# Split products for the keys and values of a sparse attention mixer, with its indexer sums on GpSimd

## The reference

```python
def dsa_mixer(h, w_in, cq_g, ckv_g, w_uq, w_uk, w_uv):
    cq, ckv, qi, ki, wi = jnp.split(h @ w_in, C_SPLITS, axis=-1)      # 384, 256, 8 x 64, 64, 8
    q = (rmsnorm(cq, cq_g) @ w_uq).reshape(b, s, C_HEADS, C_NOPE)     # 8 heads of 128
    ckv = rmsnorm(ckv, ckv_g)
    ...
    rel = jax.nn.relu(jnp.einsum('bthd,bsd->bths', qi[:, i0:end], ki[:, :end]))
    score = jnp.einsum('bths,bth->bts', rel, wi[:, i0:end])
    _, idx = lax.top_k(jnp.where(admissible, score, -jnp.inf), kk)    # 64 keys of each query
    ...                                                               # softmax over those keys, values, out
```

## Time and profile before

| | |
|---|---|
| median of 3 runs | 1085.22 us (1082.76 to 1085.29) |
| the profiled execution | 1083.29 us, span 1081.6 us |
| granted clock of TensorE, mean | 0.999 of full |
| busy share: TensorE, VectorE, ScalarE, GpSimd | 99%, 72%, 52%, 6% |

### The profile page before, as it was taken

The page is one execution under the profiler, slowest core; times in us unless marked ns, Lnnn a source line. Parts: engine busy times, 40 slices in busy tenths (PEclk is TensorE's granted clock), DMA queues, the critical chain, the costliest instruction groups (busy, mean ns, idle before and its releaser), DMA issues.

```text
span 1081.6 us, 16046 instructions
## 1 busy us (share of the span) xinstructions
PE 1070.0 (99%) x6172; PEld 938.8 (87%) x6172; DVE 776.1 (72%) x1015; ACT 565.2 (52%) x816; POOL 70.1 (6%) x169
## 2 busy tenths in 40 slices
PE   9999999999999999999999999999999999999997
PEld 8888888999888888888888888888978988888886
DVE  5966769875896786676778667677487768676675
ACT  6534446667766753353465344345466676443442
POOL 3000010010020200000010000002100101000000
PEclk9999999999999999999999999999999999999999
DMA  8746474564254365554536564553804535745641
GB/s 320 255 189 221 167 273 131 171 198 130 77 187 165 108 248 195 219 176 174 194 117 252 200 229 159 190 194 109 273 14 143 176 117 195 252 161 189 225 163 40
DMA packets 50156, 194.59 MB, mean 180 GB/s; under 512 B 4497, under 2 KB 24481, under 8 KB 31793
## 3 DMA queue, kind: packets, MB, share of 16 engines
q1 hardware_dynamic: 48832, 189.54, 49.4%
q0 software_dynamic: 1264, 4.25, 1.3%
HBM read 192.73 MB, written 1.05 MB: 179 GB/s over the span
## 4 chain that ended last, share of the span: by engine, by line
PE 91%; DVE 4%; DMA 2%; ACT 2%; issue 1%; POOL 0%; SPq 0%; POOLq 0%; DVEq 0%; ACTq 0%
PE psum L1077 22%; PE psum L961 21%; PE psum L969 11%; PE psum L942 5%; PE psum L1299 3%; PE psum L1062 3%; PE psum L947 3%; PE psum L1290 1%; PE psum L981 1%; PE psum L785 1%; PE psum L786 1%; PE psum L787 1%; PE psum L1268 1%; PE psum L1154 1%; DVE w_ring L2363 1%
## 5 line engine op out<-in xcount | busy, mean ns | idle before, releaser
L2363 DVE TENSOR_TENSOR w_ring<-raw,w_ring 128x2048 fp32r<-128x2048 f32 (+1 forms) x119 | 270.4, 2272 | 23.3 <-ACT w_ring L1665 23.0
L1665 ACT ACTIVATE w_ring<-raw 128x2048 fp32r<-128x2048 f32 x121 | 230.7, 1906 | 47.1 <-DMA raw<-in_ffn_w_gate 23.8
L2480 DVE TENSOR_REDUCE work<-psum 128x256 f32<-128x512 f32 x172 | 114.4, 686 | 175.6 <-PE psum L969 161.4
L961 PE MATMUL psum<-h_both,w_ring 128*128 128x512 f32 x1024 | 237.3, 389 | 0.0
L961 PEld LDWEIGHTS psum<-h_both,w_ring 128*128 128x128 f32 x1024 | 192.2, 188 | 39.9
L1077 PE MATMUL psum<-w_ring,g_both 128*128 128x512 f32 x936 | 220.0, 390 | 0.0
L1077 PEld LDWEIGHTS psum<-w_ring,g_both 128*128 128x128 f32 x936 | 173.2, 188 | 34.3
L1778 ACT ACTIVATE V<-work 128x512 f32<-128x512 f32 x44 | 27.9, 634 | 251.0 <-DVE work L2489 251.0
L969 PEld LDWEIGHTS psum<-h_both,w_ring 128*128 128x128 f32 x1024 | 127.1, 192 | 2.5
L969 PE MATMUL psum<-h_both,w_ring 128*128 128x256 f32 x1024 | 127.9, 283 | 0.0
L2363 DVE TENSOR_TENSOR w_ring<-QT,w_ring 128x2048 fp32r<-128x2048 f32 x40 | 91.4, 2284 | 0.8 <-ACT w_ring L1665 0.8
(11 more groups left out here) (337 smaller groups left out, 1566.5 us busy)
## 6 DMA issues: line engine op xcount, KB each, us to landing
raw<-in_ffn_w_gate SPq DMA_DIRECT2D x43, 1024.0 KB, 4.8
raw<-in_ffn_w_up SPq DMA_DIRECT2D x43, 1024.0 KB, 4.8
QT<-in_ffn_w_down SPq DMA_DIRECT2D x40, 1024.0 KB, 4.8
raw<-in_ab_w_in SPq DMA_DIRECT2D x7, 1024.0 KB, 5.5
gain_row<-in_norm_g POOLq DMA_DIRECT2D x8, 512.0 KB, 6.1
raw<-in_ffn_w_down SPq DMA_DIRECT2D x4, 1024.0 KB, 4.7
raw<-in_xa_wk SPq DMA_DIRECT2D x4, 1024.0 KB, 4.8
raw<-in_ab_w_out SPq DMA_DIRECT2D x4, 1024.0 KB, 4.8
```

Of the source, the lines that this page charges most:

```text
L961: nc.tensor.matmul(outs[-1][:, :], hi[:, k, P * j:P * (j + 1)], h_both[:, k].rearrange("p a n -> p (a n)"), start=(k == 0), stop=False)
L1665: nc.scalar.activation(w_hi[:, c % RING, 0:k * n], raw_at(c)[:, 0:k * n], ACT.Copy)\
L2363: nc.vector.tensor_tensor(w_lo[:, c % RING, 0:k * n], raw_at(c)[:, 0:k * n], w_hi[:, c % RING, 0:k * n].bitcast(F32), ALU.subtract).then_i ...
L2480: nc.vector.tensor_reduce(dst[:, p % 2, TOK * j:TOK * (j + 1)], bank(name).rearrange("p (a n) -> p n a", a=2), AX.X, ALU.add)\
```

## The change

In the sparse mixer: `cuk` and `cuv` become chunks that are split like the others, and `keys` and `latent_values` form three fp32r products with split latents (`lat_hi` by ScalarE, `key_lo` by VectorE) in place of float32 ones; the chunk of keys' and values' latent, `c.1`, comes after the indexer's and is done tile by tile. `relevance` multiplies heads in 64-row halves of the array, two halves into two banks in turn, without zeros in the key. The sums of tile 1's relevance leave VectorE for GpSimd (`relevance_sums`), as does the low split of the first output chunk, `co.0` (`first_output_lo`). The order of the units' steps on TensorE, ScalarE and VectorE is another one. In the first mixer, `abo.2`'s high split on ScalarE moves behind the copies of `qc`, and half of its low split on VectorE moves behind `hn`. At boundary 2, VectorE's split of the next feed-forward's first chunk moves from between the two halves of `gained` to between the two halves of `input_lo`.

```diff
-    uk, uv = ([A[n][0, 4 * i:4 * (i + 1)].rearrange("h (k p) n -> p (h k) n", p=P) for i in range(2)]
-              for n in ('c_w_uk', 'c_w_uv'))
-    add("ca", *uq, uk[0], split=False)
-    add("cb", uk[1], *uv, split=False)
+    uk, uv = (A[n][0].rearrange("h (k p) n -> p (h k) n", p=P) for n in ('c_w_uk', 'c_w_uv'))
+    add("ca", *uq, split=False)
+    add("cuk", uk)
+    add("cuv", uv)
...
+            def relevance_sums():
+                pool.wait_ge(const_done, 3)
+                pool.wait_ge(ki_done, 1)
+                for i in range(4):
+                    pool.wait_ge(*freed[f"rel1.{i}"])
+                    for j in range(2):
+                        link(pool.tensor_scalar(rel1[:, i, j, :], rel1[:, i, j, :],
+                                                iw[:, 1, head_of(i, j):head_of(i, j) + 1], 0.0, ALU.mult, ALU.add))
+                    link(pool.tensor_tensor(rel1[:, i, 0, :], rel1[:, i, 0, :], rel1[:, i, 1, :], ALU.add))
+                    ins = pool.tensor_tensor(score[:, 1, :], rel1[:, i, 0, :], score[:, 1, :] if i else cmask[:, 1, :],
+                                             ALU.add)
+                    if i < 3:
+                        link(ins)
+                ins.then_inc(tile1_scored, 1)
...
+            def first_output_lo():
+                c = C["co.0"]
+                pool.wait_ge(split_hi, n_split[c])
+                for q in range(4):
+                    o = slice(CH // 4 * q, CH // 4 * (q + 1))
+                    ins = pool.tensor_tensor(w_lo[:, c % RING, o], raw_at(c)[:, o], w_hi[:, c % RING, o].bitcast(F32),
+                                             ALU.subtract)
+                ins.then_inc(split_lo, 1)
+
...
+            def relevance(t, m):
                 n = P * (t + 1)
-                up(f"rel{t}.{i}", [(slice(TOK * j, TOK * j + n),
-                                    [(qiT[:, i, P * t:P * (t + 1)], kiT[:, j, 0:n])]) for j in range(2)])
-
+                outs = [take(f"rel{t}.{2 * m + j}") for j in range(2)]
+                for i in range(2):
+                    for j in range(2):
+                        o = slice(64 * j, 64 * (j + 1))
+                        last = nc.tensor.matmul(outs[j][:, TOK * i:TOK * i + n], qiT[o, 2 * m + i, P * t:P * (t + 1)],
+                                                kiT[o, 0, 0:n], start=True, stop=True)
+                        if i:
+                            filled(f"rel{t}.{2 * m + j}", last)
...
             def keys(p):
-                w = resident(f"cuk_{p // 2}").rearrange("p (h k) n -> p h k n", h=4)
-                up(f"cuk.{p}", [(slice(TOK * j, TOK * (j + 1)),
-                                 [(w[:, 2 * (p % 2) + j, k, :], latT[:, 3 + k, :]) for k in range(2)])
-                                for j in range(2)])
+                w = weights(C["cuk"])
+                three_products(f"cuk.{p}", [(slice(TOK * j, TOK * (j + 1)),
+                                             [([a[:, 2 * (2 * p + j) + n, :] for a in w], key_latent(n))
+                                              for n in range(2)]) for j in range(2)])
 
             def latent_values(i, t):
-                w = resident(f"cuv_{i}").rearrange("p (h k) n -> p h k n", h=4)
-                up(f"cuv.{i}.{t}", [(slice(0, 512), [(tile(latT[:, 3 + k, :], t), w[:, :, k, :]) for k in range(2)])])
+                w = [a.rearrange("p (h k) n -> p h k n", k=2)[:, 4 * i:4 * i + 4] for a in weights(C["cuv"])]
+                three_products(f"cuv.{i}.{t}", [(slice(0, 512), [(key_latent(n, slice(P * t, P * (t + 1))),
+                                                                  [a[:, :, n, :] for a in w]) for n in range(2)])])
```

ScalarE's and then VectorE's order of the units' steps, from the third unit's copies and from the relevance sums on:

```diff
+            prob_copy(us[2])
+            prob_copy(us[3])
+            split_to(C["co.1"])
+            exps(us[4])
+            act.wait_ge(tile1_scored, 1)
             output_hi(us[2])
-            prob_copy(us[3])
-            exps(us[4])
+            output_hi(us[3])
             split_to(C["co.2"])
-            output_hi(us[3])
+            exps(us[5])
             prob_copy(us[4])
-            exps(us[5])
+            exps(us[6])
+            output_hi(us[4])
             split_to(C["co.3"])
             prob_copy(us[5])
-            exps(us[6])
-            output_hi(us[4])
...
-            for t, i in RELEVANCE:
-                relevance(t, i)
-            top_rounds(0, range(rounds))
+            relevance(0)
+            relevance(1)
+            split_to(C["cuk"])
+            split_to(C["cuv"])
+            latent("cckv", QL, QL + KVL)
+            relevance(2)
+            relevance(3)
+            top_rounds(0, range(2))
+            key_latent_lo()
+            top_rounds(0, range(2, rounds))
             top_mask(0)
             row_max(us[0])
-            top_rounds(1, range(0, 2))
+            row_max(us[1])
             normalise(us[0])
-            row_max(us[1])
-            top_rounds(1, range(2, 4))
             normalise(us[1])
-            top_rounds(1, range(4, 6))
+            dve.wait_ge(tile1_scored, 1)
+            top_rounds(1, range(0, 6))
+            output_lo(us[0])
+            top_rounds(1, range(6, 7))
+            output_lo(us[1])
+            top_rounds(1, range(7, rounds))
             row_max(us[2])
-            output_lo(us[0])
-            top_rounds(1, range(6, rounds))
-            normalise(us[2])
-            split_to(C["co.0"])
-            output_lo(us[1])
             top_mask(1)
             row_max(us[3])
+            normalise(us[2])
             normalise(us[3])
+            row_max(us[4])
+            nxt[0] = C["co.1"]
+            dve.wait_ge(split_lo, n_split[C["co.0"]])
             split_to(C["co.1"])
+            normalise(us[4])
             output_lo(us[2])
-            row_max(us[4])
-            normalise(us[4])
             output_lo(us[3])
             row_max(us[5])
             split_to(C["co.2"])
             normalise(us[5])
             row_max(us[6])
+            output_lo(us[4])
             split_to(C["co.3"])
-            output_lo(us[4])
             normalise(us[6])
             row_max(us[7])
             output_lo(us[5])
```

The moves of the first mixer, on ScalarE and on VectorE, and that of boundary 2 on VectorE:

```diff
-            split_to(C["abo.2"])
             for i in range(2):
                 act.wait_ge(*full(f"qc.{i}"))
...
+            split_to(C["abo.2"])
             act.wait_ge(mean_done, 1)
...
-            lo_part(C["abo.2"], 1)
             dve.wait_ge(vrstd_done, 1)
...
+            lo_part(C["abo.2"], 1)
...
-                        if s == 3 and half == 0:
+                        if s in (2, 3) and half == 0:
                             split_to(last + 2)
```

223 lines of the change are left out of this document (123 added, 100 removed).

## The result

The changed kernel takes 1087.67 us (median of 11 runs, 1085.98 to 1089.72) against 1083.54 us (11 runs, 1082.49 to 1085.96) of the kernel before: a ratio of 1.0036, 95% interval 1.0027 to 1.0044. It is slower, by some 4 us. The forecast was 1084.3 us and no difference beyond 0.3% as the likeliest; the time lies within its range of 1079 to 1089, on the slow side, but it moved beyond its interval where no difference was forecast.

What follows compares the result with a forecast made beforehand. The prediction took TensorE to bound the kernel, busy 1070.0 of 1081.6 us. Sparse mixer +0.4, first mixer +0.2 and boundary 2 -0.55 summed to about 0, giving 1084.3 us, range 1079.0 to 1089.0.

Steps and rivals of the forecast that it cites:

- What leaves TensorE: Sparse mixer's keys, values, transposes and relevance products: 5.4 us less TensorE work, or 2.8 if array halves do not overlap.
- The prediction's sign for this: Relevance products at 0.06 us a record of 256 columns if the array halves overlap, 0.11 to 0.12 if not.
- The sums on GpSimd: Tile 1's relevance sums end at 792.7 to 794.7 us, about when VectorE wants them at 794.1, without a stall.
- the third rival: GpSimd's tile 1 sums end late, at 803 us, and delay VectorE's tile 1 rounds: 1087.5 to 1093 us, chance 0.17.
- The upper half: Sparse mixer up to unit 3's transpose, taken at 807.5 us: nearly all kept, 5.4 less 1 us.
- The tail's chain: ScalarE and VectorE steps from unit 3's transpose at 807.5 us to unit 5's copy at 823.9: 16.4 us.
- What the tail costs: From unit 3's to unit 6's transpose TensorE idles some 5 us, 4 ahead of unit 5's values; unit 6's transpose at 830.5.
- the mixer's +0.4: Net change of the sparse mixer: the TensorE time saved is given back by idle time in its tail, +0.4 us.
- Both of the prediction's signs of being wrong: Wait ahead of unit 5's values under 2 us: faster; VectorE's first tile 1 round waiting over 3 us on GpSimd: slower.
- The first mixer's edits: TensorE's 1.35 us wait ahead of the `qc` products goes, but `raw` is freed later: +0.2 us, from -1.0 to +0.6.
- Boundary 2: TensorE's wait for `x_state` behind a split, ahead of 368.36 us, goes: -0.55 us.
- The sum: Sparse mixer +0.4, first mixer +0.2 and second boundary -0.55 us: about 0, so 1084.3 us.

Runs made afterwards that it cites:

- repairs_one_half: Changed kernel with unit 5's copy earlier, `co.0`'s low split later, first mixer's moves undone, all relevance products on rows 0 to 63: 1082.43 us, ratio 0.9992.
- late_low_split: Changed kernel with GpSimd's low split of `co.0` held until unit 1's probabilities are normalised: 1086.48 us, ratio 1.0017 to the kernel before.
- copy_ahead: Changed kernel with unit 5's copy on ScalarE ahead of unit 6's exponentials, `output_hi` of unit 4 and `co.3`'s high split: 1082.49 us, ratio 0.9986.
- rows_ahead: Changed kernel with unit 2's output rows back between unit 4's values and unit 5's transposes on TensorE: 1082.09 us, ratio 0.9986.
- fill_wait: Changed kernel with seven extra, unused float32 products in TensorE's wait ahead of unit 5's values: 1086.04 us, ratio 1.0021.

## Why the prediction was wrong

**What leaves TensorE**: right in kind, 1.3 us too large. Values take 1.47 us a call (forecast 1.37), two calls of keys 787.46 to 790.52, 1.53 each (1.44), and the four 6.0 together. The relevance products take 0.134 a record of 256 columns where 0.11 was assumed: three rows of the changed kernel,

```profile
772.37 0.72 PE L1556 MATMUL psum<-krT,shared 64*128 64x128 f32 x8
...
783.89 1.13 PE L1556 MATMUL psum<-krT,shared 64*128 64x256 f32 x8
784.96 2.86 PE L1331 MATMUL psum<-latT,w_raw 128*128 128x256 f32 x12
```

the last of them the start of what follows. Together all eight items take 3.4 us, so 2.0 are saved of the 2.7 taken; in all 0.9 + 0.9 + 0.2 + 2.0, some 4.1 in place of 5.4. The prediction's sign for this does not fit its own sum: the sum takes 0.11 us a record of 256 columns with the halves side by side (half of 0.22), while the sign says 0.06 for that case and 0.11 to 0.12 for halves one after the other. Read by the sign, 0.134 would have meant that they do not overlap; `repairs_one_half`, at 0.24 on one half, shows that they do. The Trainium skill, "TensorEngine Tiling (Array Packing)", "Performance Considerations", puts a contract dimension of 64 down for twofold row tiling; here two halves are 1.8 times as fast as one.

**The sums on GpSimd**: right, and the third rival falls. They end at 793.17 us; with the kernel's later start of 1.0 us that is 792.2 against 792.7. A two-input operation takes 0.73 us, a TENSOR_SCALAR 0.53.

**The upper half**: too early by 1.5 us at unit 3's transpose (810.00, so 809.0, against 807.5). The tile 1 rounds start at 797.31, 796.3 without the start's 1.0, against 794.1. The step that failed is "`co.0`'s low split on GpSimd, four pieces after the sums, ends by 800 to 804 and is wanted at 807.5": it is in time (798.5), but holds up VectorE's normalisations. `late_low_split` puts that at 1.0 us of the mixer's time. What is left comes from TensorE's own rows, which save less than forecast: with no wait at all, they would have brought it to that transpose some 1.6 us later than the forecast's 806.4.

**The tail's chain**: right. From unit 3's transpose (810.00) to unit 5's values (826.04) it took 16.04 us; forecast were 16.4, with 4 us of waiting, measured 3.67.

**What the tail costs**: here the prediction failed. The step is "Then unit 5's values and one group of output rows, together 3.71 (826.43 to 830.14), and the other group, 2.8, which gives 830.5": it prices the work behind a stall of 4 us at the full clock. It took 9.15 in place of 6.5 us, 2.65 more. `copy_ahead`, `rows_ahead` and `fill_wait` each bring the full clock back and this time with it. With the 1.5 us from above and 0.4 less in the chain, the mixer's +0.4 becomes +4.15; measured are +4.05. Both of the prediction's signs of being wrong, a wait under 2 us and a first tile 1 round more than 3 us late for GpSimd, stayed away: neither looked at the pace behind the wait.

**The first mixer's edits**: +0.2 was forecast with an upper end of +0.6; it is +1.0 in the profile, +0.6 in the mean of six profiles, and +2.3 in the one where the clock fell. The late chunk was seen, but priced as barely late. **Boundary 2**: -0.55 forecast, -0.5 measured.

The sum with these sizes: +4.05 + 0.6 - 0.5 = some +4.1 us, the measured difference of medians. That the time still lies in the stated range is luck: its upper end was set by late sums on GpSimd, which did not happen.

## What to carry to other kernels

A stall on the engine that bounds the kernel has two prices: its length, and the slower clock of the work behind it, here 2.7 us for a wait of 3.7, and 1.6 for one of 3.0. A forecast that leaves the bounding engine idle for some microseconds in one piece should count both, so work that can wait belongs into such a gap, and is not to be put behind it. When an engine is given work off the critical path, ask whom it blocks while it runs, not only whether it ends in time. And what one engine's written order puts ahead of a short copy (here a 1.9 us split and exponentials) decides more than the copy: one line moved on ScalarE was worth 5 us.

## What the runs showed of the hardware

- The granted clock fell to its lower level in the changed kernel (0.50 from 825 to 831 us, behind TensorE's idle time from 822.4 on) and in each of the three other profiles with one wait of 3 us or more in this mixer (3.67, 3.00 and 5.42 us); it stayed at 1.00 there in the others, where no wait is over 1.2 us. Behind waits of 1.2 to 2.4 us in the first mixer it fell in one profile of six (2.13 us in `fill_wait`; 2.40 us in the changed kernel, without a fall). The Trainium skill, "TensorE: Matmul & The Clock Gate", Part 1, names TensorE's recent activity as what sets this clock, which `fill_wait` bears out.
- Float32 products on 64 rows of the array take 0.24 us a record of 256 columns on one half and 0.134 with both in use, also when two neighbours use the same half, against 0.23 on the whole array.
- GpSimd's two-input operation in float32: 0.73 us for 128x256; for 128x512 1.35 beside VectorE's normalisations, 1.41 beside its sums (5.64 us for four) and 1.25 beside the tile 1 rounds (4.99 us for four).
- VectorE is held up by GpSimd as GpSimd is by VectorE: a normalisation of 128x256 took 1.40 us in place of 0.42, seven sums of the same size 7.20 us where three took 1.53 before.
